# Attention gate and last recurrent quarter from three rounded products per tile, with the gate rows in another order

## The reference

```python
mod = silu(c) @ w_ada + b_ada
shift, scale, gate = split(mod, 3)
h = rms_norm(x) * (1 + scale) + shift
xr, gr, qc, kvc, kr, ga = split(h @ w_in)      # 1024, 1024, 512, 512, 64, 1024 columns
y_rnn = rg_lru(conv4(xr)) * silu(gr)
y_att = mla(qc, kvc, kr) * silu(ga)            # 8 heads, 128 + 64 rotary dimensions
x = x + gate * (concat(y_rnn, y_att) @ w_out)
```

## Time and profile before

| | |
|---|---|
| median of 3 runs | 2692.35 us (2692.2 to 2693.52) |
| profiled execution | 2691.99 us, of which the profile's span is 2689.8 |
| PE busy | 2679.5 us (100%) |
| PEld | 2348.9 us (87%) |
| DVE | 1977.5 us (74%) |
| ACT | 1197.8 us (45%) |
| DMA | 528.18 MB, mean 196 GB/s |
| chain of waits | PE 97%, DVE 2%, ACT 1% |

### The profile page before, as it was taken

One profiled execution on the slowest core, in us unless ns is written; L12 is line 12 of the kernel. 1 busy time (PEld: TensorE's weight loads), 2 busy tenths in 40 slices (PEclk: granted clock), 3 DMA queues, 4 the chain that ended last, 5 costly groups with the idle time before them and its releaser, 6 DMA issues.

```text
span 2689.8 us, 44167 instructions
## 1 busy us (share of the span) xinstructions
PE 2679.5 (100%) x15336; PEld 2348.9 (87%) x15336; DVE 1977.5 (74%) x2594; ACT 1197.8 (45%) x1533; POOL 5.7 (0%) x12
## 2 busy tenths in 40 slices
PE   9999999999999999999999999999999999999999
PEld 7888888888888888888888888888888888888888
DVE  6747577777777788667787776699878876688865
ACT  2004354555555444444444443366544444444443
POOL 0000000000000000000000000000000000000000
PEclk9999999999999999999999999999999999999999
DMA  9986665555556666666666666644566666666664
GB/s 342 366 278 191 205 192 191 165 174 163 160 164 196 188 195 190 198 190 195 189 194 188 196 200 190 188 157 140 181 188 195 196 191 192 192 190 195 196 202 155
DMA packets 705780, 528.18 MB, mean 196 GB/s; under 512 B 32221, under 2 KB 694559, under 8 KB 705439
## 3 DMA queue, kind: packets, MB, share of 16 engines
q1 hardware_dynamic: 701872, 523.73, 63.9%
q10 hardware_dynamic: 3823, 3.31, 0.4%
HBM read 523.80 MB, written 2.10 MB: 196 GB/s over the span
## 4 chain that ended last, share of the span: by engine, by line
PE 97%; DVE 2%; ACT 1%; issue 0%; DMA 0%; DVEq 0%; SPq 0%; ACTq 0%
PE acc L707 80%; PE acc L845 3%; PE acc L1039 2%; PE acc L833 2%; PE turned L845 2%; PE sums L845 2%; PE mixed L960 1%; PE sums L1191 1%; DVE pro_ada L1915 0%; DVE wr L1841 0%; PE scores L1184 0%; PE sums L745 0%; PE mixed L961 0%; PE sums L916 0%; PE scores L946 0%
## 5 line engine op out<-in xcount | busy, mean ns | idle before, releaser
L707 PE MATMUL acc<-stream,wr 128*128 128x512 f32 (+1 forms) x7680 | 1328.4, 333 | 0.3 <-DVE wr L1841 0.3
L707 PEld LDWEIGHTS acc<-stream,wr 128*128 128x128 f32 x7680 | 1159.1, 188 | 156.0 <-issue 3.8
L1841 DVE TENSOR_TENSOR wr<-raw,wr 128x1024 fp32r<-128x1024 f32 x832 | 998.5, 1222 | 318.2 <-ACT wr L1367 308.6
L1367 ACT ACTIVATE wr<-raw 128x1024 fp32r<-128x1024 f32 x832 | 871.1, 1058 | 693.8 <-PE acc L707 678.1
L707 PE MATMUL acc<-ys,wr 128*128 128x512 f32 (+1 forms) x4264 | 732.4, 332 | 1.0 <-DVE wr L1841 0.9
L707 PEld LDWEIGHTS acc<-ys,wr 128*128 128x128 f32 x4264 | 642.7, 188 | 85.3 <-DVE wr L1841 1.5
L707 PE MATMUL acc<-wr,stream 128*128 128x512 f32 (+1 forms) x1024 | 182.7, 338 | 0.0
L707 PEld LDWEIGHTS acc<-wr,stream 128*128 128x128 f32 x1024 | 157.0, 188 | 22.5 <-issue 0.5
L1725 ACT ACTIVATE ffn_cv<-ffn_cv 128x256 f32<-128x256 f32 x88 | 36.9, 419 | 245.4 <-DVE ffn_cv L2459 245.4
L1851 DVE TENSOR_REDUCE ffn_ug<-acc 128x512 f32<-128x1024 f32 x88 | 107.8, 1225 | 35.3 <-PE acc L707 35.3
L1874 DVE TENSOR_TENSOR ys<-tmp,ys 128x256 f32 (+3 forms) x108 | 51.2, 474 | 76.0 <-ACT ys L1373 73.4
(11 more groups left out here) (334 smaller groups left out, 1546.1 us busy)
## 6 DMA issues: line engine op xcount, KB each, us to landing
raw<-in_ffn_w_up SPq DMA_DIRECT2D x704, 256.0 KB
raw<-in_ffn_w_down SPq DMA_DIRECT2D x160, 512.0 KB
raw<-in_a_w_qkv SPq DMA_DIRECT2D x96, 512.0 KB
raw<-in_b_w_kv SPq DMA_DIRECT2D x64, 512.0 KB
aring<-in_w_ada SPq DMA_DIRECT2D x96, 256.0 KB, 6.6
w<-in_w_in SPq DMA_DIRECT2D x48, 512.0 KB
raw<-in_w_ada SPq DMA_DIRECT2D x32, 512.0 KB, 5.1
raw<-in_w_out SPq DMA_DIRECT2D x32, 512.0 KB
```

What stands on the lines that cost most here:

```text
L707: mm = pe.matmul(*ops, start=first and ops is wide, stop=last and ops is wide)
L1367: f(half_of(0, s), raw[:, s, :], ACT.Copy)\
L1841: tt(half_of(1, s), raw[:, s, :], half_of(0, s), ALU.subtract).then_inc(T.unit_split[s].sem, 1)
```

## The change

The 20 units of the recurrent gate's last quarter and of the attention gate no longer go to PE as 8 float32 products but as 24 rounded ones, from a high and a low part of the weights and of `xm`:

```diff
+            def three_products(out, high, low, j, k, k0, first, last):
+                cols = slice(j * P, (j + 1) * P)
+                x_high, x_low = xm_high[:, k0 + k, :], xm_low[:, k0 + k, :]
+                pe.matmul(out, high[:, k, cols], x_high, start=first, stop=False)
+                pe.matmul(out, high[:, k, cols], x_low, start=False, stop=False)
+                return pe.matmul(out, low[:, k, cols], x_high, start=False, stop=last)
...
-                            mm = pe.matmul(bank(b + j)[:, 0:TOK], w[:, k, j * P:(j + 1) * P], xm[:, u * UK + k, :],
-                                           start=u == 0 and k == 0, stop=u == 3 and k == UK - 1)
+                            mm = three_products(bank(b + j)[:, 0:TOK], high, low, j, k, u * UK, u == 0 and k == 0,
+                                                u == 3 and k == UK - 1)
```

ACT makes the high part of a unit in another place of `w1`, DVE subtracts it in place; PE waits for `low_out`. The ring is cut into eight places for these units, five for the loaded (then low) part and three for the high part:

```diff
+LOW_PLACES, HIGH_PLACES = [5, 6, 0, 1, 2], [7, 4, 3]
...
+                    act.wait_ge(F.w1_in[n % ONE_RING].sem, UNIT * (n // ONE_RING + 1))
+                    act.wait_ge(F.w1_used.sem, HIGH_FREE[n])
+                    f(high_tiles(n), unit_tiles(n), ACT.Copy).then_inc(F.high_out.sem, 1)
...
+                    dve.wait_ge(*F.high_out.next())
+                    tt(low_tiles(n), unit_tiles(n), high_tiles(n), ALU.subtract).then_inc(F.low_out.sem, 1)
```

**xm** is split into `xm_high` (ACT, in the memory of `h`) and `xm_low` (DVE, over `xm`). So ACT sends `h` to DRAM after unit 27, and SP loads it back in four pieces behind the first pair of `w_out`, each when one of the last units is done; DVE waits for it before `residual_product`:

```diff
+            act.wait_ge(F.w1_used.sem, QUARTER_AT[2])
+            act.dma_start(h_kept, h[:, :, :]).then_inc(F.h_kept.sem, 16)
+            act.wait_ge(F.h_kept.sem, 16)
...
+                if n == 0:
+                    for u in range(4):
+                        tiles_back = slice(u * UK, (u + 1) * UK)
+                        sp.wait_ge(F.w1_used.sem, ONE_UNITS - 3 + u)
+                        sp.dma_start(h[:, tiles_back, :], h_kept[:, tiles_back, :]).then_inc(F.h_back.sem, 16)
```

**Gate rows.** All 32 now come before the heads, with the sums in two buffers; PE's `gate_sums(0)` moves from the fourth slot between the units to the first, `gate_sums(1)` from the twentieth to the eleventh. DVE's order:

```diff
+            gate_row(4)
+            for u in range(3):
+                xm_lows(u)
+            gate_row(4)
             lora_out("q")
             rnn_in(0)
+            gate_row(2)
             lora_out("kv")
+            gate_row(2)
             rope_key()
...
             rnn_in(3)
+            xm_lows(3)
             for n in range(N_U + 2):
+                if n >= N_U:
+                    low()
...
-                    gate_row()
-                if n >= N_U:
-                    gate_row()
+                    gate_row(2 if n >= 10 else 1)
...
-            for i in range(4):
+            for i in range(3):
+                low()
                 rnn_gate(i)
...
+                if hd == 0:
+                    rnn_gate(3)
...
-                gate_row()
-                gate_row()
+                low(2 if hd < 7 else 1)
```

More of the change, by code:

```diff
@@ L81 @@
 ONE_SPAN, _at = [], 0
-for _n in range(ONE_UNITS):
+for _n in range(GR_AT):
     _lora = _n < XR_AT and not any(q <= _n < q + 8 for q in QUARTER_AT)
     _size = LORA_COLS if _lora else UK * 256
-    if _n == ONE_UNITS - 8:
-        _at = ONE_SPACE // 2
     if _at + _size > ONE_SPACE:
@@ L550, in gate_load, with recurrent_load @@
                   .then_inc(F.gate_in[n % RING].sem, 16)
+            def recurrent_load():
+                sp.wait_ge(F.rgw_zeroed.sem, 1)
+                for m, name in enumerate(("w_rg_a", "w_rg_x")):
+                    for b in range(2):
+                        r = slice(64 * b, 64 * b + 64)
+                        sp.dma_start(rgw[r, m, :, r], t[name][0].rearrange("(t b) i j -> b i t j", b=2)[b])\
+                          .then_inc(T.rgw_in.sem, 16)
             for r in range(KT):
@@ L585, in _ @@
                 lora_load(k)
-            sp.wait_ge(F.rgw_zeroed.sem, 1)
-            for m, name in enumerate(("w_rg_a", "w_rg_x")):
-                for b in range(2):
-                    r = slice(64 * b, 64 * b + 64)
-                    sp.dma_start(rgw[r, m, :, r], t[name][0].rearrange("(t b) i j -> b i t j", b=2)[b])\
-                      .then_inc(T.rgw_in.sem, 16)
+            for _ in range(RING):
+                gate_load()
             for i in range(4):
                 quarter_load(i, 3)
-            for what, g in U_PAIRS:
+                if i >= 2:
+                    gate_load()
+            for n, (what, g) in enumerate(U_PAIRS):
                 if what in ("nope", "rope"):
@@ L999, in _ @@
             rope_turn(kpe[:, :], 1, 0)
-            pe.wait_ge(T.rgw_in.sem, 64)
             for n, (what, g) in enumerate(U_PAIRS):
+                if what == "v" and g == 0:
+                    pe.wait_ge(T.rgw_in.sem, 64)
                 if g == 0:
@@ L1029, in _ @@
             for i in range(4):
-                two_tiles(halves(take(GR_BANK[i])), xm, 3 * UK)
+                out = halves(take(GR_BANK[i]))
+                high, low = split_unit()
+                for j in range(2):
+                    for k in range(UK):
+                        mm = three_products(out(j), high, low, j, k, 3 * UK, k == 0, k == UK - 1)
+                mm.then_inc(F.w1_used.sem, 1)
                 attention(i)
@@ L2129, in _, with gate_row, next_row @@
             gate_rows = [0]
-            def gate_row():
+            def gate_row(count=1):
+                for _ in range(count):
+                    next_row()
+            def next_row():
                 n = gate_rows[0]
@@ L2140, in gate_row, with xm_lows, low @@
                 if r == 0:
-                    w = ts(gate_sum[:, :], raw[:, n % RING, :], c, None, ALU.mult)
+                    w = ts(here, raw[:, n % RING, :], c, None, ALU.mult)
                 else:
                     own(T.gate_used)
-                    w = stt(gate_sum[:, :], raw[:, n % RING, :], c, gate_sum[:, :], ALU.mult, ALU.add)
+                    w = stt(here, raw[:, n % RING, :], c, here, ALU.mult, ALU.add)
                 w.then_inc(*T.gate_used.one())
+            def xm_lows(u):
+                tiles = slice(u * UK, (u + 1) * UK)
+                dve.wait_ge(F.high_ready.sem, u + 1)
+                tt(xm_low[:, tiles, :], xm[:, tiles, :], xm_high[:, tiles, :], ALU.subtract)
+            low_units = [GR_AT]
+            def low(count=1):
+                for _ in range(count):
+                    n = low_units[0]
+                    low_units[0] += 1
+                    dve.wait_ge(*F.high_out.next())
[4 more added lines that the diff above has]
+            gate_row(4)
             lora_out("q")
             rnn_in(0)
+            gate_row(2)
             lora_out("kv")
+            gate_row(2)
             rope_key()
```

77 lines of the change are left out of this document (60 added, 17 removed).

## The result

The changed kernel takes 2700.86 us (median of 8 runs, 2698.83 to 2701.78) against 2692.85 us before (8 runs, 2692.2 to 2693.52): a ratio of 1.0029 with a 95% interval of 1.002 to 1.0038. That is 8 us more, just beyond the range's upper end of 2700.

What follows compares the result with a forecast made beforehand. PE was taken to bound the rewritten stage; -14.6 + 4.4 + 1.5 + 1.4 + 4.4 + 1.7 + 2.2 = +1.0 us against the profiled 2691.99 gave 2693 us, with a range of 2686 to 2700.

Steps and rivals of the forecast that it cites:

- (a): Rotary key: PE waits for it behind gate rows 10 and 11 and row 11's late load; +4.4 us, bounds 4.0 and 9.6.
- (c): Query heads: last tile difference and row 12 ahead of the first head delay ACT's third square, which PE needs; +1.4 us.
- (d): First gate unit: PE waits for its difference behind rows 25 to 27, load 25 being late; +4.4 us, bounds 2.9 and 8.5.
- (b): Convolutions behind the key on DVE: PE waits for the bank of the third recurrent unit; +1.5 us.
- (e): Third and sixth gate units: PE waits 0.8 and 0.9 us for late differences; +1.7 us together.
- (f): The heads: DVE and ACT wait for each other in a ring that holds up PE; +2.2 us, bounds 0 and 5.4.
- rival 2: The clock falls in PE's waits at the key and first gate unit: +5.0 us, 2698, or +10, 2703; chance 0.20.
- A clock under 1.00 behind the gaps: Sign of a wrong forecast: granted clock below full speed behind PE's waits at the key and first gate unit.
- units of 2.83 us and more: Sign of a wrong forecast: attention gate units on PE this long, where a pitch near 2.72 us was expected.
- at nothing: Costs taken as 0: moved gate sums, loading h back, and writing h out, the last between 0 and 5.6 us.
- the term of the products: Attention gate: 480 rounded products at 113.5 ns replace float32 ones, 14.6 us less PE, bounds 12.5 and 17.3.
- rival 3: Gate products: the distance of 112 between weights and tiles does nothing, 117.9 ns each, +2.1 us, 2695; chance 0.08.

Runs made afterwards that it cites:

- e2: The changed kernel with gate rows 10 and 11 moved from ahead of the rotary key to the latents' units; 2693.78 us.
- e5: The changed kernel with e2's edits, row loads 25 to 31 ahead of unit 61 on SP, and the last tile difference behind the third query head; 2686.13 us.
- e1: The changed kernel with 12 extra unused PE products ahead of the rotary key's turn and 8 ahead of the first gate unit; 2698.4 us.
- e4: The changed kernel without writing h to DRAM, pieces of w_out being loaded back in its place; 2699.12 us.
- e6: The changed kernel with the units' places at 0 modulo 256 instead of 208; 2697.4 us.
- e12: The kernel before the change with only the units' places moved, to 208 modulo 256 instead of 0; 2693.48 us.
- e7: The changed kernel with the units' places at 192 modulo 256 instead of 208; 2700.06 us.
- e11: The changed kernel with the units' places at 128 modulo 256 instead of 208; 2699.77 us.
- e13: e8 with the second gate sums behind the last quarter's fourth unit, and the tiles at 80 modulo 256 instead of 64; 2683.47 us.
- e14: e13 with the units' places at 16 modulo 256 as well; 2685.71 us.
- e10: e8 with the second gate sums moved earlier, one 512-column product replacing two of 256, and the high-weight, low-tile product left out of the sum; 2683.3 us.
- e3: The changed kernel with row loads 25 to 28 ahead of unit 61 on SP instead of behind it; 2698.05 us.
- e8: The changed kernel with the edits of e5 and e6 together; 2683.22 us.

## Why the prediction was wrong

**(a), (c) and (d) were right in mechanism and near in size:** 5.5, 1.4 and 3.9 us against 4.4, 1.4 and 4.4, released as foreseen, and gone when the rows and loads were moved (e2, e5). The key's wait was longer because row 11's load took 213.33 - 207.94 = 5.4 us to land, where I took 4.0 and had bounds to 9.2. (b) was 0 because PE came to that bank slowly, not because DVE was early: in e1, at full clock, it reappears with 0.82. (e) and (f), forecast at 3.9 together, cost about 1.2: the stage gained 9.8, and twenty units at 2.91 on average instead of 3.46 gain 11.0. The sixth unit waited 0.50 where 0.9 was forecast, the third not at all, and in the heads PE waited twice, 0.55 and 0.2.

**The step that failed first is the clock: the sum has no term for it, and rival 2, which had the price nearly right, was judged too unlikely.** I gave "the clock falls in the two waits" 0.20, with the argument that no row of this kernel shows it. But no row could: PE never stopped in that stage, so the rows spoke neither for nor against. It happened in all executions of the change (mean clock 0.997 or 0.998 in each), at 2.3 us and 1.8 us against the 2.5 that I had worked out from the earlier trace rows; what e1 got back of it is 2.5 us. A clock under 1.00 behind the gaps was one of the prediction's own signs of being wrong; units of 2.83 us and more, here 2.92, were another. The rule of the Trainium skill (TensorE: Matmul & The Clock Gate, Part 1: The HAM clock gate), that an idle PE is throttled and activity releases it, was the better guide: the trace agrees, with 0.50 behind waits of 5.5 and 3.9 us.

**The second is a term that the sum did not have.** The part on costs "at nothing" took 0 for the writing of `h`, with 5.6 us as its upper bound, and looked at the units' new place only as a distance to the tiles. That place took the rate of the stretch from 356 to 343 GB/s and, with the writing, cost 3.1 us before the key (e4, e6, e12). My argument was that DVE was idle there; the row beside it, a DMA share of 1.10, was the one that mattered.

**The third is the term of the products, mis-sized:** 14.6 us forecast, 11.0 measured, under even the lower bound of 12.5. I took 113.5 ns from an average over long and short products and gave it to the short ones because of the same distance of 112. The other row at hand, the last product with three short products and 117.9 ns, has the gate's form and was the right one: the gate's products come 118 ns apart. Of the 1.5 us that are left some 1.2 are the slower start of each of the 14 pieces (0.20 us to the second product instead of 0.118). That the distance does nothing was rival 3, at 0.08; e6, e7, e11, e13 and e14 show 118 ns at every place. Why the main product reaches 113 is not settled: neither the places tried nor the mix of lengths (e10) gives it.

Put together: 1.1 for the key, 4.1 for the clock, 3.6 before the key, 3.6 for the products and 0.7 in the main product and 0.3 elsewhere, less 1.5 for (b), 0.5 for (d) and 2.7 for (e) and (f), are the 8.7 us between forecast and measurement. The terms are not independent: the slow clock behind the key and the missing (b) nearly cancel, as e1 shows. And that the total came within 1 us of the range's end is in part luck, as (b), (e) and (f) were forecast 4.2 us too high together.

## What to carry to other kernels

A load that is issued behind a wait on a queue makes everything behind its consumer late, and moving the consumer away from the critical row, as in e2, or the load ahead of the wait, as in e3 and e5, each take one line; look for the second such place before counting the gain of the first. A new wait on PE can cost more than its length, since the clock may fall behind it, unless the slow stretch lies where another engine is late anyway. Where a buffer moves, ask the loads first and the products second: the place that was chosen for PE's reads gave nothing there and took some 3.5% of the bandwidth in a stretch whose DMA share is over 1.

## What the runs showed of the hardware that I had not expected

- With the units (most of their rows 1 KB and more) at 0 modulo 256 the DMA moved 353 to 356 GB/s over 92 us, with them at 16, 128, 192 and 208 it moved 342 to 346, though less than half of the bytes went there.
- The clock can fall without a wait: in one of e8's five executions it was 0.62 over 4 us in which PE was busy throughout, behind 16 products of one column, and 0.78 at the same point in e7's profile. And it can fall behind a short wait: 0.78 behind 1.90 us in e1, where it stayed at 1.00 behind 1.20 us in the change.
- Rounded products of 256 columns came 118 ns apart in the gate, whatever their places, with 0.20 us between the first two of a piece, and took 113 ns in the main product of the same trace.
